# Weights laid out by the host in the order of use, loaded two pieces at a time

## The reference

```python
for layer in range(DEPTH):                      # 2
    shift, scale, gate = jnp.split((cond @ w_ada[layer] + b_ada[layer])[:, None, :], 3, axis=-1)
    h = rms_norm(x, norm_g[layer]) * (1.0 + scale) + shift
    (qkv_a, z_a, beta_raw, alpha_raw, glu_in, z_b, q_c, k_c, v_c, z_c,
     q_i, k_i, w_i, gate_raw) = split_columns(h @ w_in[layer])
...
    merged = (g_a * (y_a @ w_proj_a[layer]) + g_b * (y_b @ w_proj_b[layer])
              + g_c * (y_c @ w_proj_c[layer]))
    x = x + gate * (merged @ w_out[layer])
```

## Time and profile before

| | us |
|---|---|
| median of 3 runs (2207.5 to 2211.78) | 2210.04 |
| span of the profiled execution | 2204.9 |
| TensorE busy | 2140.4 |
| GpSimd busy | 1664.8 |
| VectorE busy | 1225.2 |
| ScalarE busy | 959.7 |

### The profile page before, as it was taken

The page is one execution under the profiler, slowest core; times in us unless marked ns, Lnnn a source line. Parts: engine busy times, 40 slices in busy tenths (PEclk is TensorE's granted clock), DMA queues, the critical chain, the costliest instruction groups (busy, mean ns, idle before and its releaser), DMA issues.

```text
span 2204.9 us, 37807 instructions
## 1 busy us (share of the span) xinstructions
PE 2140.4 (97%) x14842; PEld 1949.9 (88%) x14842; DVE 1225.2 (56%) x2153; ACT 959.7 (44%) x1056; POOL 1664.8 (76%) x676
## 2 busy tenths in 40 slices
PE   5799999999999999999989999999999999999999
PEld 3789999988879988788989999999788998888899
DVE  6859974847655455544562894756667455430110
ACT  3334444483333544444344344446633354444442
POOL 1558858767765898998868886877667679998876
PEclk7889999999999999999999999999999999999999
DMA  9978646545553699898975775555545458966754
GB/s 363 382 266 233 182 126 183 162 138 159 158 157 115 218 353 340 295 340 310 350 256 172 195 211 147 170 163 150 156 148 158 133 182 306 350 206 202 223 192 153
DMA packets 228987, 479.59 MB, mean 218 GB/s; under 512 B 22096, under 2 KB 26448, under 8 KB 220272
## 3 DMA queue, kind: packets, MB, share of 16 engines
q1 hardware_dynamic: 228688, 477.54, 67.1%
q10 hardware_dynamic: 160, 0.13, 0.0%
HBM read 471.19 MB, written 6.29 MB: 217 GB/s over the span
## 4 chain that ended last, share of the span: by engine, by line
PE 42%; POOL 30%; issue 23%; DVE 3%; ACT 1%; DVEq 1%; POOLq 0%; ACTq 0%
POOL wl L539 30%; PE ps L940 13%; PE ps L941 13%; PE ps L942 13%; DVE score L1632 1%; PE ps L1302 0%; ACT wh L560 0%; POOLq L538 0%; PE ps L1309 0%; PE ps L1290 0%; PE ps L1236 0%; ACTq L737 0%; PE ps L1225 0%; PE ps L1258 0%; PE ps L1252 0%
## 5 line engine op out<-in xcount | busy, mean ns | idle before, releaser
L539 POOL TENSOR_TENSOR wl<-raw,wh 128x1024 fp32r<-128x1024 f32 x672 | 1664.6, 2491 | 527.1 <-ACT wh L560 525.4
L560 ACT CAST wh<-raw 128x1024 fp32r<-128x1024 f32 x672 | 703.8, 1050 | 1118.2 <-PE ps L942 871.9
L940 PE MATMUL ps<-ah,wh 128*128 128x256 f32 x3008 | 867.7, 288 | 24.1 <-DVE al L1502 14.9
L941 PE MATMUL ps<-al,wh 128*128 128x256 f32 x3008 | 856.5, 285 | 0.0
L942 PE MATMUL ps<-ah,wl 128*128 128x256 f32 x3008 | 856.1, 285 | 0.0
L940 PEld LDWEIGHTS ps<-ah,wh 128*128 128x128 f32 x3008 | 583.0, 194 | 30.5 <-DVE al L1502 15.2
L941 PEld LDWEIGHTS ps<-al,wh 128*128 128x128 f32 x3008 | 583.2, 194 | 3.9 <-issue 3.6
L942 PEld LDWEIGHTS ps<-ah,wl 128*128 128x128 f32 x3008 | 582.8, 194 | 0.0
L940 PE MATMUL ps<-wh,ah 128*128 128x512 f32 (+1 forms) x832 | 319.8, 384 | 0.9 <-POOL wl L539 0.9
L942 PE MATMUL ps<-wh,al 128*128 128x512 f32 (+1 forms) x832 | 317.1, 381 | 0.0
L941 PE MATMUL ps<-wl,ah 128*128 128x512 f32 (+1 forms) x832 | 317.0, 381 | 0.0
(11 more groups left out here) (280 smaller groups left out, 1702.7 us busy)
## 6 DMA issues: line engine op xcount, KB each, us to landing
raw<-w_in SPq DMA_DIRECT2D x512, 512.0 KB, 3.7
modw<-w_ada SPq DMA_DIRECT2D x64, 1024.0 KB, 7.8
adaw<-w_ada SPq DMA_DIRECT2D x64, 512.0 KB, 8.5
raw<-w_out SPq DMA_DIRECT2D x64, 512.0 KB, 5.2
raw<-w_pc SPq DMA_DIRECT2D x32, 512.0 KB, 3.8
raw<-w_pb SPq DMA_DIRECT2D x32, 512.0 KB, 6.3
raw<-w_pa SPq DMA_DIRECT2D x32, 512.0 KB, 4.8
gbias<-b_gate SPq DMA_DIRECT2D x24, 256.0 KB, 4.3
```

Source lines behind the costliest of these rows:

```text
L539: nc.gpsimd.tensor_tensor(wl[:, s], raw[:, s], wh[:, s].bitcast(F32), ALU.subtract).then_inc(sem("w_split"), 1)
L560: A.copy(wh[:, s], raw[:, s]).then_inc(sem("w_rounded"), 1)
L940: M.matmul(o, lh, rh, start=start, stop=False, skip_group_check=True)
L941: M.matmul(o, lh, rr, start=False, stop=False, skip_group_check=True)
```

## The change

The host writes all weight pieces of a layer in the order of use into one array, w_piece, in which two neighbouring pieces form a row of 8 KB for each partition. stream issues one transfer of 1 MB for two pieces, into two neighbouring slots, at the even piece, and nothing at the odd one. It waits until both slots are free, that is for one split more than the single piece waited for; one semaphore stands for each pair of slots. The same is done for the first blocks of w_ada (w_first, one transfer of 1 MB in place of two of 512 KB) and for the columns of ki, wi, beta and alpha (w_misc, one transfer in place of two with short rows). Slots, the casts, the splits and the matmuls stay as they are.

```diff
+for _n, _s, _g in (("glu", 4, G_IN), ("qc", 2, G_IN), ("kc", 1, G_IN), ("qi", 1, G_IN), ("qkv", 6, G_IN), ("zc", 2, G_IN),
+                   ("gate_c", 4, G_IN), ("proj_c", 4, G_PR), ("zb", 2, G_IN), ("za", 2, G_IN),
+                   ("gate_b", 4, G_IN), ("proj_b", 4, G_PR), ("gate_a", 4, G_IN), ("proj_a", 4, G_PR),
+                   ("out", 4, G_IN)):
+    PIECE[_n] = (_at, _g)
+    _at += _s * _g
...
-        raw_landed = [sem(f"raw_landed{n}") for n in range(RING)]
+        raw_landed = [sem(f"raw_landed{n}") for n in range(RING // 2)]
...
-                for part in (SHIFT, SCALE):
-                    col = part * D + q * GW
-                    sp.dma_start(adaw[j % 4][:, :, part], wa[0, :, 2 * j:2 * j + 2, col:col + GW]
-                                 ).then_inc(ada_landed[j % 4], 16)
+                sp.dma_start(adaw[j % 4][:], w_first[n]).then_inc(ada_landed[j % 4], 16)
...
-                            sp.dma_start(mraw[:, :, 0:IDIM + HEADS],
-                                         wi[layer, :, :, COL["ki"]:COL["ki"] + IDIM + HEADS]
-                                         ).then_inc(sem("misc_landed"), 16)
-                            sp.dma_start(mraw[:, :, IDIM + HEADS:MISC],
-                                         wi[layer, :, :, COL["beta"]:COL["beta"] + 2 * HEADS]
+                            sp.dma_start(mraw[:], w_misc[layer].rearrange("p (k n) -> p k n", n=MISC)
                                          ).then_inc(sem("misc_landed"), 16)
...
-                def stream(src, col, k0, hc, slot):
+                def stream(name, g, j, hc, slot):
+                    at, n = PIECE[name]
+                    if j % 2:
+                        return
                     if hc >= RING:
-                        sp.wait_ge(sem("w_split"), hc - RING + 1)
-                    sp.dma_start(raw[:, slot], src[layer, :, k0:k0 + HK, bass.ds(col, GW)]
-                                 ).then_inc(raw_landed[slot], 16)
+                        sp.wait_ge(sem("w_split"), hc - RING + 2)
+                    sp.dma_start(raw[:, slot:slot + 2], w_piece[layer, (at + g * n + j) // 2]
+                                 ).then_inc(raw_landed[slot // 2], 16)
...
-                    act.wait_ge(raw_landed[s], uses * (16 // RING) + 16)
+                    act.wait_ge(raw_landed[s // 2], uses * (16 // RING) + 16)
```

More of the change, by code:

```diff
@@ L68 @@
 HCL = 36 * G_IN + 12 * G_PR
+GATE = {"a": 0, "b": 1, "c": 2}
+PIECE = {}
+_at = 0
+for _n, _s, _g in (("glu", 4, G_IN), ("qc", 2, G_IN), ("kc", 1, G_IN), ("qi", 1, G_IN), ("qkv", 6, G_IN), ("zc", 2, G_IN),
[4 more added lines that the diff above has]
+    _at += _s * _g
+assert _at == HCL
 PAR = {}
@@ L137, in bucket_rows, with trunk @@
     return hot
-def trunk(nc, xt, cvec, rel_bias, w_ada, w_in, w_pa, w_pb, w_pc, w_out, b_gate, params, consts, hot, out):
+def trunk(nc, xt, cvec, rel_bias, w_ada, w_first, w_piece, w_misc, b_gate, params, consts, hot, out):
     ctx = ExitStack()
@@ L409, in _ @@
                 hc = h0
-                first, second = COL["glu"], COL["glu"] + CW
                 if layer == 0:
-                    chunks = [(col, j) for q in range(4) for col in (first, second, first + GW)
-                              for j in range(2 * q, 2 * q + 2)]
+                    chunks = [(g, j) for q in range(4) for g in range(3) for j in range(2 * q, 2 * q + 2)]
                     def chunk(n):
-                        col, j = chunks[n]
-                        stream(wi, col, j * HK, n, n % RING)
+                        g, j = chunks[n]
+                        stream("glu", g, j, n, n % RING)
                     for n in range(32):
@@ L431, in _ @@
                     hc += 24
-                    group(wi, second + GW, hc)
+                    group("glu", 3, hc)
                     hc += G_IN
@@ L435, in _ @@
                     for i in range(2):
-                        group(wi, first + i * GW, hc)
+                        group("glu", 2 * i, hc)
                         if i == 0:
                             store(layer - 1)
-                        group(wi, second + i * GW, hc + G_IN)
+                        group("glu", 2 * i + 1, hc + G_IN)
                         hc += 2 * G_IN
@@ L505, in turn @@
                             units2 = {0: lambda: load(2), 3: lambda: load(3)}
-                        group(wi, i * GW + (COL["gate"] + GATE[br] * D), i * TURN + hc, units=units)
+                        group("gate_" + br, i, i * TURN + hc, units=units)
                         sp.wait_ge(sem("gbias_free"), i + (12 * layer + 4 * "cba".index(br) + 1))
@@ L524, in _ @@
                             units[j] = lambda kt=kt: mod_load(layer + 1, SCALE, kt, passes[2] + kt, kt % 2)
-                    group(wo, i * GW, i * G_IN + hc, units=units)
+                    group("out", i, i * G_IN + hc, units=units)
                 hc += 4 * G_IN
@@ L2100, with tiled @@
         params[:, :, o:o + s] = a.transpose(1, 0, 2)
+    def tiled(w, col, n):
+        w = f(w)
+        k = w.shape[1] // (HK * P)
+        w = w[:, :, col:col + n * GW].reshape(DEPTH, k, HK, P, n, GW)
+        return w.transpose(0, 4, 1, 3, 2, 5).reshape(DEPTH, n * k, P, HK * GW)
+    glu = tiled(w_in, COL["glu"], 4).reshape(DEPTH, 2, 2, G_IN, P, HK * GW).transpose(0, 2, 1, 3, 4, 5)
+    blocks = [glu.reshape(DEPTH, 4 * G_IN, P, HK * GW)]
+    blocks += [tiled(w_in, COL[n], g) for n, g in (("qc", 2), ("kc", 1), ("qi", 1), ("qkv", 6), ("zc", 2))]
+    blocks += [tiled(w_in, COL["gate"] + GATE["c"] * D, 4), tiled(w_proj_c, 0, 4), tiled(w_in, COL["zb"], 2),
+               tiled(w_in, COL["za"], 2), tiled(w_in, COL["gate"] + GATE["b"] * D, 4), tiled(w_proj_b, 0, 4),
+               tiled(w_in, COL["gate"] + GATE["a"] * D, 4), tiled(w_proj_a, 0, 4), tiled(w_out, 0, 4)]
+    w_piece = np.concatenate(blocks, axis=1).reshape(DEPTH, HCL // 2, 2, P, HK * GW).transpose(0, 1, 3, 2, 4)
+    w_piece = np.ascontiguousarray(w_piece.reshape(DEPTH, HCL // 2, P, 2 * HK * GW))
+    first = f(w_ada)[0, :, :2 * D].reshape(KT // 2, 2, P, 2, 4, GW).transpose(4, 0, 2, 1, 3, 5)
+    w_first = np.ascontiguousarray(first.reshape(4 * KT // 2, P, 2, 2, GW))
+    misc = np.concatenate([f(w_in)[:, :, COL["ki"]:COL["ki"] + IDIM + HEADS],
+                           f(w_in)[:, :, COL["beta"]:COL["beta"] + 2 * HEADS]], axis=2)
+    w_misc = np.ascontiguousarray(misc.reshape(DEPTH, KT, P, MISC).transpose(0, 2, 1, 3).reshape(DEPTH, P, KT * MISC))
     xt = np.ascontiguousarray(f(x)[0].T.reshape(KT, P, T).transpose(1, 0, 2).reshape(P, KT * T))
     arrays = {"xt": xt, "cvec": np.ascontiguousarray(f(c)[0].reshape(KT, P).T), "rel_bias": f(rel_bias),
-              "w_ada": f(w_ada), "w_in": f(w_in), "w_pa": f(w_proj_a), "w_pb": f(w_proj_b), "w_pc": f(w_proj_c),
-              "w_out": f(w_out), "b_gate": f(b_gate), "params": params, "consts": constants(), "hot": bucket_rows()}
+              "w_ada": f(w_ada), "w_first": w_first, "w_piece": w_piece, "w_misc": w_misc, "b_gate": f(b_gate), "params": params, "consts": constants(), "hot": bucket_rows()}
     nc = bacc.Bacc("TRN2", target_bir_lowering=False, num_devices=1)
```

26 lines of the change are left out of this document (10 added, 16 removed).

## The result

The changed kernel takes **2231.64 us** (median of 4 runs, 2230.94 to 2233.58) against 2208.77 before (4 runs): ratio **1.0106, 95% [1.0092, 1.0120]**, some 23 us slower. The prediction was 2212, its range ended at 2228: it was wrong, with the direction of rival C and more than rival C's size. The profiled execution has a span of 2229.3 us, 24.4 more than before's 2204.9.

A forecast was written before the change was run, and what follows sets the result against it. TensorE was taken as the bound, busy 2140.4 of 2204.9 us. Terms 3 + 0 - 0.9 + 0 = +2.1 us gave a span of 2207; 5.1 us carried over to measured time made 2212, range 2201 to 2228.

The forecast's parts named there:

- rival C: Token turns with modulation loads: two splits and one 1 MB load make the ring fall behind; +12 us, 2222; chance 0.34.
- A: Whole kernel, the forecast: nothing to be measured, the ring stays level with TensorE; 2212 us, range 2206 to 2216; chance 0.41.
- layer 0, turns of b and a: 96 pieces, 24 loops beside modulation loads: loop 0.37 us over TensorE's pace, 8.9 us less cushion; +3 us, 0 to +12.
- The price of one transfer: Weight loads: 1 MB lands after 4.9 us against 3.5 for 512 KB, so 512 KB more costs 1.4 us.
- The loop: Ring refill, load, cast to split and two splits: 10.8 us per four pieces, 11.25 in layer 0 beside modulation.
- The pace: TensorE's use of four pieces: 10.88 us in the token turns, 11.52 us where channels are on the partitions.
- The cushion takes 4.6 of it: Layer 0's token turns: pieces ready 4.6 us before TensorE wants them, taken off the 8.9 us loss.
- The rest: Remaining stages, including the load of x before w_out, the small-column load and bias tables: 0, from -2.5 to +4 us.
- The start: First blocks of w_ada: shorter VectorE waits, -2.3 us, and a later pair behind skew stores, +1.4; net -0.9 (-5 to +4).
- Layer 1: 12 loops of b lose less than the cushion, the 12 of a have no modulation loads: 0, up to +5 us.
- At the layer's change: Change of layer: no new idle time expected; idle time appearing there would show the prediction wrong.
- Rival B: Larger rows pay: adaw waits, idle to 1045 us and about 1 us at layer's end go; -8 us, 2202; chance 0.25.

## Why the prediction was wrong

*The mechanism was rival C's, the forecast was A's.* Load, cast, two splits, and no send before the second: loads of 4.8 us (forecast 4.9) make 4.8 + 1.13 + 2 x 2.38 = 10.7 us, level with TensorE's 10.88. What failed is how I turned a loop that is level into a time.

*Failed step: layer 0, turns of b and a, "+3 us", between 0 and +12.* Measured 19.5 - 7.4 = **+12.1** by the splits and 19.7 - 6.2 = +13.5 by TensorE's end, at its upper bound or over it. ScalarE waited for each of the 48 pairs, as forecast, but TensorE's idle time to 1045 was 10.5 us and not 6. The price of one transfer held: the loads averaged 5.10 us (forecast 5.05). Three other terms were mis-sized.

- *The loop.* Means over these 48 pairs of the trace: load 5.10, landing to cast 0.09, cast to split 1.33, the two splits 2.50 and 2.63, the end of the second to the next send 0.03. With 0.04 us of overlap that is 11.64 us, where I had 11.25; by the time the 96 pieces took, 1061.8 - 778.7 = 283.1 us, it is 11.8 for four. Half of the missing 0.4 us is cast to split: behind a slow split of one pair, GpSimd is late for the other pair's cast too (up to 2.9 us in place of 1.13). I had counted a slow split once, and the hand-overs at nothing.
- *The pace.* With half a split, pairs, and no gap in TensorE, the same 96 pieces take 266.4 us, 11.1 for four. I had taken 10.88 from the interval of two casts. Before already took 271.0 us, 11.3 for four, so 4.6 us of this kind of loss were in it.
- *"The cushion takes 4.6 of it".* It wasn't there. I had read the 43 late casts for w_in and left out the rows beside them. From 770 to 1045 us of before:

```profile
ACT wh L560 <- PE ps L942: 39.7, 26, 2.8
ACT wh L560 <- DMA raw<-w_pa: 28.9, 15, 6.0
ACT wh L560 <- DMA raw<-w_pb: 12.8, 8, 3.0
```

With the 43 that is 66 casts that waited for these weights and 26 that waited for TensorE. At piece 208 TensorE was done 6.1 us after the split's end in before and 4.9 in the changed kernel, against 3.4 and 3.6 at piece 304, where nothing is left: a cushion of 2.7 and of 1.3 us. From 777.62 on ScalarE waited for every pair.

Every pair was late here, so the mean loop times 24 is the time, and a mean was the right tool; no cushion may be taken off it that the kernel before has spent too. By its own terms the forecast also stood next to rival C: that rival's 0.4 us over the pace needs loads of 5.08 us and not the 5.2 named, and the forecast had 5.05.

*Failed step: "The rest", 0.* Before the turns of b, TensorE was already 6.2 us late. Of this, 3.3 us arose in the first turn of c (2.9 us late at piece 128, 6.2 at piece 140, and no more until piece 208). I had argued that the loop has room there. It has, and yet the pairs cost time. GpSimd's timeline, before and then the changed kernel:

```profile
501.61 17.70 POOL L539 TENSOR_TENSOR wl<-raw,wh 128x1024 fp32r<-128x1024 f32 x7 [3.22 <-ACT wh L560]
```

```profile
504.56 10.48 POOL L539 TENSOR_TENSOR wl<-raw,wh 128x1024 fp32r<-128x1024 f32 x4 [3.22 <-ACT wh L560]
516.27 4.76 POOL L539 TENSOR_TENSOR wl<-raw,wh 128x1024 fp32r<-128x1024 f32 x2 [1.23 <-ACT wh L560]
```

After ScalarE had been away at the branch's own work, single pieces refill at GpSimd's rate, seven splits in a row. Pairs give four, which are the four slots, and then a gap. But that gap doesn't reach TensorE: from 162 to 764 us it never waits for a split in the changed kernel. The one wait of TensorE in that window that differs, before and then the changed kernel:

```profile
PE ps L1236 <- DVE xm L1849: 1.1, 1, 1.1
```

```profile
PE ps L1236 <- DVE xm L1849: 2.8, 1, 2.8
```

TensorE waits for VectorE, 1.7 us longer, because one operation of the delta rule now runs beside a split and takes 2.47 us in place of 0.28 (its rows are in the last section). Behind that wait the granted clock is at 1.2 GHz for 3.4 us, which costs another 1.7. The same operation is slow (2.4 to 2.5 us) in the profiled runs with two transfers at the pair's time (TensorE waits 3.8 us), with pairs in the old layout (2.9) and with pairs and the old first blocks (3.0). In none of those that send single pieces one by one it is, with whole splits (1.1). What the pairs changed is the moment at which the splits fall; I had no term for that.

*Failed step: "The start", -0.9.* The new wait before 70 us is there (1.27 us, forecast 1.7). The wait at 99.15 was to shrink to 0.3 and is 2.17. VectorE in the changed kernel, to set against the earlier trace rows:

```profile
69.74 1.29 DVE L1429 SCALAR_TENSOR_TENSOR ps<-adaw,cond,ps 128x1024 f32<-128x1024 f32 x1 [1.27 <-DMA adaw<-w_first]
...
99.15 1.29 DVE L1429 SCALAR_TENSOR_TENSOR ps<-adaw,cond,ps 128x1024 f32<-128x1024 f32 x1 [2.17 <-DMA adaw<-w_first]
...
128.10 1.28 DVE L1429 SCALAR_TENSOR_TENSOR acc<-adaw,cond,ps 128x1024 f32<-128x1024 f32 x1
```

The last product came at 128.10, not near 126; the single-piece version, whose blocks don't queue behind pairs, has 125.80. The larger loss is behind it. ScalarE's casts in the changed kernel after the start, for the earlier trace rows, and then the first matmul on piece 24, before and in the changed kernel:

```profile
153.48 1.99 ACT L560 CAST wh<-raw 128x1024 fp32r<-128x1024 f32 x2 [7.02 <-DMA raw<-w_piece]
...
165.43 2.00 ACT L560 CAST wh<-raw 128x1024 fp32r<-128x1024 f32 x2 [4.83 <-DMA raw<-w_piece]
...
176.13 2.00 ACT L560 CAST wh<-raw 128x1024 fp32r<-128x1024 f32 x2 [4.71 <-DMA raw<-w_piece]
```

```profile
155.30 0.39 PE L940 MATMUL ps<-ah,wh 128*128 128x256 f32 x1 [1.28 <-POOL wl L539]
```

```profile
157.00 0.39 PE L940 MATMUL ps<-ah,wh 128*128 128x256 f32 x1 [3.50 <-POOL wl L539]
```

The +1.4 us for the pair behind the stores was right (1.7 measured at piece 24's split). But TensorE waited 2.2 us longer for it, and behind the wait the granted clock was at 1.2 GHz for 3.4 us, from 158.5 on, where before it was at 2.4; that costs 1.7 us and was in no term. TensorE was then 3.2 us late. The ring stayed empty for a while (the split of piece 32 is 5.4 us late, and before the casts were TensorE's again from 164.29 on), yet TensorE lost no more up to piece 128: there the 0.7 us to spare that I had counted were enough.

*Layer 1.* Turns of b and a +2.2 us by TensorE's end (24.3 - 22.1; forecast 0, up to +5); no gap from 1980 to 2090, as forecast. The turns of c cost 2.4 us again: TensorE waits 1.9 us in place of 1.1 for the same line of VectorE, where another operation (L1837) takes 2.26 us in place of 1.48 beside a split, and 3.4 us at 1.2 GHz follow.

*At the layer's change* idle time was to stay the same. TensorE even made up 1.8 us over the 32 pieces of w_out (in that stage the clock was low for 3.4 us less than before), and had lost them again by the turns of c of layer 1.

*The part of the loss that is not idle time.* TensorE's idle time grew by 14.9 us, its busy time by 9.5. Windows of 10 us, before and then the changed kernel:

```profile
530.00:540.00 10.00, 10.00 (x92) 8.12 (x92) 6.32 (x9) 2.64 (x4) 5.85 (x3) 1.00 0.47 125
1610.00:1620.00 10.00, 10.00 (x49) 8.43 (x49) 7.87 (x55) 3.84 (x4) 8.11 (x4) 1.00 0.52 158
```

```profile
530.00:540.00 10.00, 10.00 (x70) 7.68 (x67) 3.19 (x7) 2.09 (x2) 4.22 (x2) 0.83 0.39 130
1610.00:1620.00 10.00, 9.44 (x87) 7.24 (x88) 2.35 (x8) 3.00 (x3) 4.55 (x3) 0.83 0.38 138
```

After TensorE waited in a turn of c, in each layer, the granted clock was 0.83 on average in a stretch of 10 us (about a third of it at 1.2 GHz) where before it was at the full 2.4 GHz. Over all windows of 10 us up to 2200 us, 10 us times what the granted clock lacks of full comes to 35.9 us against 32.4. So about 3.5 of the 9.5 us are clock. The other 6 stay open.

*Rival B* was right about the first blocks with single pieces (2.7 us) and wrong about the pieces. The Trainium skill's rule in "DMA: Bandwidth & Descriptors" (Rules for kernel authors), at least 1 MiB per DMA for the most bandwidth, would have picked the slower kernel. The trace doesn't contradict what it says of bandwidth: 512 KB more cost 1.4 us. But this kernel waits for latency in a ring of four slots, and has bandwidth to spare.

*What is shown and what isn't.* That the pairing costs, and not the layout or the order, is shown by runs that change one thing: the late send costs 17 us, the later landing 13, and short splits remove the loss. By stage the loss of the profiled execution is 2.9 us at the start, 3.3 and 2.4 in the turns of c, 13.5 and 2.2 in the turns of b and a, and nothing net in between. In layer 0's turns of b and a about 9 of 12 us hang on the slow splits. The other 3 aren't split between late landings and the queue, and the step at the turns of c is read from traces; no run moved the splits away from that operation.

## What to carry to other kernels

A ring of buffers is a loop: load, plus every step until the slot is free again, times the pieces that must be done before the next send. Put two slots in one transfer and the send waits a step longer and the first use waits for the last byte; compare that loop with the consumer's pace, both taken from the stage in question. Put every hand-over and every slow step into the mean, also for the neighbour that waits behind the slow one, and take no cushion off it before counting how many of the first engine's starts already wait for a transfer. And look at what the new moments of the splits fall beside: two losses here came by an operation that shared its time with a split. Coalesce where transfers are consumed whole and nothing waits a slot longer (the first blocks here, 2.7 us with single pieces), and keep the small transfer where depth is counted in slots; a host layout with longer rows gave 3.5 us here with single pieces and 12.4 with pairs.

## What the hardware showed that I had not expected

- Three times fewer packets (73816 against 228987) and a share of the DMA engines of 57.7% on the main queue instead of 67.1% came with a kernel 23 us slower.
- A small VectorE operation beside a GpSimd split can take nearly nine times as long. One execution of L1842 (two operands in SBUF) in the first turn of c, before and then the changed kernel, min/median/max ns:

```profile
L1842 DVE TENSOR_TENSOR wq<-qkv,egr x1: 279/279/279, 522.3 to 522.3; 128x128 f32<-128x128 f32 x1
```

```profile
L1842 DVE TENSOR_TENSOR wq<-qkv,egr x1: 2469/2469/2469, 524.7 to 524.7; 128x128 f32<-128x128 f32 x1
```

Before, it began 0.05 us ahead of the next split; in the changed kernel it began 0.33 us after one had begun (524.38) and ended 0.15 us after that split's end (527.03). TensorE's next step of the delta rule waited 2.8 us for VectorE in place of 1.1. The Trainium skill, "GPSIMD Engine Reference" (section Specifications), names this contention, for VectorE instructions with two SBUF inputs among others; the trace agrees and gives the size. Whether a split meets such an operation depends on where the pieces have slid to.
- Half of the split's columns is worth 14.5 us to the kernel before (2207.71 to 2193.16), although TensorE was 97% busy. VectorE's busy time fell with it from 1225.2 to 1124.0 us at the same 2153 instructions, which fits the same contention seen from the other side.
